# The last stores of a two-layer encoder trunk, issued by row halves from two engines

## What is computed

```python
def reference(x, p, ...):
    for i in range(DEPTH):                      # DEPTH = 2
        z = _rmsnorm(x, pre_norm_g[i]) @ w_in[i]
        ...                                     # both attentions, gated: oa, ob
        y = jnp.concatenate([oa * jax.nn.silu(ga), ob * jax.nn.silu(gb)], axis=-1) @ w_out[i]
        x = x + _rmsnorm(y, post_norm_g[i])
        gate = jax.nn.sigmoid(x @ w_ple_gate[i])
        e = (p[i] @ w_ple_proj[i]) * gate
        x = x + _rmsnorm(e, ple_norm_g[i])
    return x                                    # (1, 256, 1024) f32, 1 MB
```

## Time and profile before

| | before |
|---|---|
| median of 3 runs | 357.34 us (357.05 to 357.71) |
| the profiled execution | 356.97 us |
| its span, from first to last instruction | 355.2 us |
| around the span | 1.77 us |
| TensorE busy | 347.7 us, 98% of the span |
| granted TensorE clock, mean | 0.994 of full speed |
| DMA, mean over the span | 172 GB/s, 61.12 MB |
| of it written to memory | 1.05 MB |

### The profile page before, as it was taken

The page is one execution under the profiler, slowest core; times in us unless marked ns, Lnnn a source line. Parts: engine busy times, 40 slices in busy tenths (PEclk is TensorE's granted clock), DMA queues, the critical chain, the costliest instruction groups (busy, mean ns, idle before and its releaser), DMA issues.

```text
span 355.2 us, 5701 instructions
## 1 busy us (share of the span) xinstructions
PE 347.7 (98%) x1927; PEld 291.6 (82%) x1927; DVE 263.2 (74%) x562; ACT 228.9 (64%) x459; POOL 68.1 (19%) x121
## 2 busy tenths in 40 slices
PE   8999999999999999999999999999999999999992
PEld 7887888888888788888888888888888888888882
DVE  3886979988765776786697487998897458678543
ACT  4897566777578955555757564788666795465221
POOL 1076540142200000013106534014220000000000
PEclk9999999999999999999999999999999999999997
DMA  8996797662753364657575926546356346550011
GB/s 291 380 339 203 78 315 231 176 179 66 215 190 124 122 224 128 223 149 156 181 227 159 352 89 200 159 120 187 109 164 194 119 127 230 177 171 9 2 49 69
DMA packets 31820, 61.12 MB, mean 172 GB/s; under 512 B 2376, under 2 KB 4432, under 8 KB 31792
## 3 DMA queue, kind: packets, MB, share of 16 engines
q1 hardware_dynamic: 30656, 57.48, 49.9%
q0 software_dynamic: 1120, 3.28, 5.1%
q10 hardware_dynamic: 16, 0.00, 0.0%
HBM read 59.71 MB, written 1.05 MB: 171 GB/s over the span
## 4 chain that ended last, share of the span: by engine, by line
PE 96%; issue 2%; DVE 1%; ACT 0%; POOLq 0%; DVEq 0%; POOL 0%
PE proj L1256 25%; PE proj L1258 25%; PE proj L1257 25%; PE sc L1337 3%; PE tr L1407 2%; PE tr L1355 2%; PE pv L1424 2%; PE sc L1189 1%; PE proj L1173 1%; PE proj L1200 1%; PE pv L1429 1%; PE proj L1189 1%; PE pv L1189 1%; PE proj L1162 1%; PE sc L1207 1%
## 5 line engine op out<-in xcount | busy, mean ns | idle before, releaser
L1256 PE MATMUL proj<-w_hi,act_hi 128*128 128x512 f32 (+1 forms) x392 | 157.1, 401 | 0.0
L1258 PE MATMUL proj<-w_hi,act_lo 128*128 128x512 f32 (+1 forms) x392 | 152.2, 388 | 0.0
L1257 PE MATMUL proj<-w_lo,act_hi 128*128 128x512 f32 (+1 forms) x392 | 151.6, 387 | 0.0
L854 DVE TENSOR_TENSOR w_lo<-raw,w_hi 128x1024 fp32r<-128x1024 f32 (+1 forms) x102 | 121.2, 1209 | 14.3 <-ACT w_hi L612 13.7
L612 ACT ACTIVATE w_hi<-raw 128x1024 fp32r<-128x1024 f32 (+2 forms) x103 | 102.3, 1023 | 2.6 <-PE proj L1258 1.8
L1258 PEld LDWEIGHTS proj<-w_hi,act_lo 128*128 128x128 f32 x392 | 73.6, 188 | 15.5
L1256 PEld LDWEIGHTS proj<-w_hi,act_hi 128*128 128x128 f32 x392 | 73.7, 188 | 14.1 <-issue 0.7
L1257 PEld LDWEIGHTS proj<-w_lo,act_hi 128*128 128x128 f32 x392 | 73.9, 188 | 12.9
L552 POOL TENSOR_TENSOR rstd<-var,minus_half 128x1 f32<-128x1 f32 x12 | 7.6, 640 | 190.1 <-DVE var L842 161.4
L748 ACT ACTIVATE probs<-probs,neg_max 128x128 f32<-128x128 f32 (+1 forms) x64 | 28.2, 443 | 5.2 <-DVE neg_max L1005 5.2
L542 POOL TENSOR_TENSOR v_all<-work,rot_tab 128x128 f32<-128x128 f32 x16 | 10.6, 662 | 76.0 <-ACT work L612 75.8
(11 more groups left out here) (225 smaller groups left out, 455.6 us busy)
## 6 DMA issues: line engine op xcount, KB each, us to landing
raw<-in_w_in_dram SPq DMA_DIRECT2D x59, 512.0 KB, 4.3
raw<-in_w_out_dram SPq DMA_DIRECT2D x16, 512.0 KB, 3.4
raw<-in_w_ple_gate_dram SPq DMA_DIRECT2D x16, 512.0 KB, 3.7
raw<-in_w_in_dram SPq DMA_DIRECT2D x7, 324.0 KB, 5.5
raw<-in_w_ple_proj_dram SPq DMA_DIRECT2D x4, 512.0 KB, 3.9
resid<-in_x_dram SPq DMA_DIRECT2D x2, 512.0 KB, 6.6
probs<-in_w_in_dram SPq DMA_DIRECT2D x2, 512.0 KB, 9.3
g_ple<-in_ple_norm_g_dram POOLq DMA_DIRECT2D x2, 512.0 KB, 5.2
```

The costliest lines, as they stand in the source:

```text
L854: nc.vector.tensor_tensor(w_lo[:, g % SLOTS, 0:nk * cols], landing(g, nk * cols), w_hi[:, g % SLOTS, 0:nk * cols].bitcast(fp32), ALU.subtr ...
L1256: nc.tensor.matmul(ps, src_hi[:, b, k0 + k, :], hi, start=(first_u and k == 0), stop=False)
L1257: nc.tensor.matmul(ps, src_hi[:, b, k0 + k, :], lo, start=False, stop=False)
L1258: last = nc.tensor.matmul(ps, src_lo[:, b, k0 + k, :], hi, start=False, stop=last_k)
```

## The change

The two stores of row block 1 are cut in two by rows. The sync engine stores partitions 0 to 63 (rows 128 to 191) of each column half, and ScalarE stores partitions 64 to 127 (rows 192 to 255) from its own DMA queue, at the end of its list, each after a wait for the same count of `x2_done`. A new semaphore, `stored_low`, counts ScalarE's two stores, and the sync engine waits for it after `stored`. The stores of block 0 are as before.

```diff
-        eg_done, stored = sem("eg_done"), sem("stored")
+        eg_done, stored, stored_low = sem("eg_done"), sem("stored"), sem("stored_low")
@@ sync engine
             for i in range(2 * NB):
                 b, n = divmod(i, 2)
                 sp.wait_ge(x2_done, (DEPTH - 1) * 4 + i + 1)
-                sp.dma_start(out[0, b * P:(b + 1) * P, n * N:(n + 1) * N], resid[:, b, n * N:(n + 1) * N])\
+                rows = P if b == 0 else P // 2
+                sp.dma_start(out[0, b * P:b * P + rows, n * N:(n + 1) * N], resid[0:rows, b, n * N:(n + 1) * N])\
                     .then_inc(stored, 16)
             sp.wait_ge(stored, 16 * 2 * NB)
+            sp.wait_ge(stored_low, 16 * 2)
@@ ScalarE, in its list of steps
+                elif kind == "last":
+                    for n in range(2):
+                        act.wait_ge(x2_done, L * 4 + 3 + n)
+                        nc.scalar.dma_start(out[0, P + P // 2:2 * P, n * N:(n + 1) * N],
+                                            resid[P // 2:P, 1, n * N:(n + 1) * N]).then_inc(stored_low, 16)
```

## The result

| | before | after |
|---|---|---|
| median | 357.36 us (356.73 to 357.71, 6 runs) | 358.53 us (357.84 to 358.75, 6 runs) |
| ratio of the times | | 1.0031, 95% interval 1.0016 to 1.0046 |
| the profiled execution | 356.97 us | 357.84 us |
| its span | 355.2 us | 356.0 us |
| tail: end of VectorE's last update to end of span | 355.16 - 352.70 = 2.46 us | 356.00 - 352.65 = 3.35 us |

The changed kernel is slower by 0.3%, 0.6 to 1.6 us by the interval. The forecast was 357.36 us with a range up to 358.0, and "slower by over 0.2%" had a chance of 0.10.

The account below looks back on a forecast made before the run. TensorE holds 96% of the 355.2 us span; the change reaches only the 2.5 us tail of stores. Terms -0.02 + 0 + 0 + 0.02 + 0.02 + 0 = +0.02 us on 357.34 gave 357.36 us, range 356.95 to 358.0.

Parts of the forecast that it names:

- (4): Block 1's stores: four transfers have 64 small packets instead of 32; +0.02 us, bounds 0 and 0.04.
- (6): Final barrier: ScalarE's drain starts later but the wait for the sync engine covers it; 0, without cover 0.54 us.
- (5): Kernel end: the sync engine's additional wait; +0.02 us, bounds 0 and 0.05.
- (1): Sync engine's block 1 issues shrink from 128 rows to 64, so the first packet comes earlier; -0.02 us, bounds -0.04 and 0.
- (3): Block 1's store data: same bytes on the same full DMA engines, 0; a half alone at half rate costs 0.12 us more.
- half-rate rival: Block 1's half-row transfers run at half rate, one queue after the other; +1.37 us, 358.7 us, chance 0.08.
- (2): ScalarE issues the other halves of block 1, starting level with the sync engine; 0, at worst +0.24 us.
- late ScalarE: Rival: ScalarE's block 1 stores are late, the last half landing 0.24 to 0.36 us later; 357.6 to 357.7 us, chance 0.12.

Follow-up runs that it names:

- e2: Against the kernel before: block 1 stored as four transfers of 64 neighbouring rows, all from the sync engine; 358.76 us, ratio 1.0043, tail 3.98 us.
- e12: Against the kernel before: block 1 stored by the sync engine as 48, 80, 64 and 64 rows; one profiled execution, tail 3.58 us.
- e1: The changed kernel unaltered, run again and compared with the kernel before; 358.60 us, ratio 1.0034, tail 3.47 us.
- e5: Against the kernel before: block 1 stored as four transfers of 64 even or odd rows, all from the sync engine; 358.77 us, ratio 1.0032, tail 3.89 us.
- e8: The changed kernel with row halves swapped (sync engine partitions 64 to 127, ScalarE 0 to 63); 358.65 us, ratio 1.0040 to the kernel before, tail 3.47 us.
- e9: The changed kernel with even rows from the sync engine, odd rows from ScalarE; 357.72 us, ratio 1.0014 to the kernel before, tail 3.08 us.
- e10: The changed kernel with only ScalarE's half of block 1 stored, rows 128 to 191 left out; one profiled execution, data 1.40 us at 187 GB/s.
- e3: Against the kernel before: block 1's second column half, all 128 rows, stored by ScalarE, the first by the sync engine; 357.49 us, ratio 0.9999, tail 2.57 us.
- e4: Against the kernel before: both column halves of block 1, 128 rows each, stored by ScalarE; 357.63 us, ratio 1.0004, tail 2.59 us.
- e6: Against the kernel before: block 1 stored as four transfers of 128 rows by 256 columns, all from the sync engine; 358.13 us, ratio 1.0017, tail 3.05 us.
- e7: Against the kernel before: block 1 stored as four transfers of 128 rows by 256 columns, by sync engine and ScalarE; 357.74 us, ratio 1.0008, tail 2.76 us.

## Why the prediction was wrong

**What held.** The reading of the tail (2.5 us, all of it behind VectorE's last update), and parts (4) and (6): the data end 0.83 us before the end of the span before and 0.88 after. ScalarE's drain starts at 353.5 and is over long before the barrier. (5) can't be told apart. Two of the prediction's own signs of being wrong came: about 200 GB/s while one queue alone was moving, and queue 10's first packet 0.6 us behind queue 1's.

**Part (1) had the wrong sign.** The step from "128 rows are 332 ns, 256 rows are 367 ns" to "64 rows save 18 ns" took a straight line through two points and went on below them. An issue of 64 rows takes 548 ns (e2, e12). The first packet follows about 1.2 us after the issue's start in seven profiles (after, e1, e2, e5, e8, e9, e10) and 0.83 to 0.87 us with 128 rows (before, e3, e4, e6, e7). I had -0.02 us with bounds of -0.04 and 0; it was +0.36, and it alone takes half of the 0.71 us that I called invisible. The longer issue is 548 - 332 = 216 ns of it. The other 0.15 us lie behind the issue's end, where the first packet comes after 0.65 us with 64 rows and after 0.50 with 128 (before, e4); the prediction had no term for that.

**Part (3) and the half-rate rival were treated as an either-or.** I priced half rate at +1.37 us for all four transfers in turn, gave it 0.08, and let it go with the remark that two halves side by side fill each other's gaps. In the changed kernel they are not side by side at the start: queue 10 began only as queue 1's half ended, as the lines by queue show. My evidence for mixing was one stretch of the opening, in which one of the two transfers was 4 KB. So the first half went alone at 201 GB/s, and the last one, with nothing left beside it, ended alone at 215. In between the rate was mostly 380 to 420. The cost is +0.48 us of data, and e9, which has all of the change but the neighbours, has +0.03. I had only 0.12 for it, in part (3), as a bound. Why the halves in the middle escape I can only argue: by then both queues hold packets for different partitions, so the reads of one may run ahead under the other's. e2 (199 GB/s) and e10 (187), where no other queue is there, are slow from end to end, which fits.

**Part (2).** The late ScalarE was a wrong worry as put, since its 575 ns is no property of a queue long unused (e3, e4). It was late for another reason: its packets waited for the slow half of queue 1, and its last landing came after 2.9 us. Its second issue took 786 ns, but that is not seen to cost anything: in e9 it takes 799 and no gap follows.

**The sum.** +0.36 for the first packet (64 rows), +0.48 for the data (neighbours) and +0.05 behind them. That is 0.89 us of tail. The measured 1.17 us of the medians has an interval of 0.6 to 1.6 and doesn't contradict it.

**The chances.** Two costs, each under 0.71 us, add up to more than that. I weighed each rival alone against the threshold and gave no chance to a bit of two of them. The range's upper end of 358.0 came from one late store and should have added the half-rate stretches.

No run beat the kernel before. e3 and e4 tie with it: the issuing engine is free to choose, the cut isn't.

## What to carry to other kernels

A store at the end of a kernel is a lag, a stretch of data and a landing; if the data of one transfer already hide the issue of the next, a second issuer has nothing to save. Best don't cut it; if it must be cut, do it by columns and keep all 128 partitions, which cost 0.30 us with two issuers and 0.59 with one. A part of the partitions, if they are neighbours, draws about half the rate when no other queue runs beside it, and 64 rows were slower to issue than any other number tried. A price for a new shape of transfer doesn't come from a line through two other shapes; where no row has the shape, the bounds must reach to the slowest issue in the trace.

## What the runs showed of the hardware

- 64 rows of 2 KB: an issue of 0.52 to 0.61 us from either engine, neighbours or strided (0.57 to 0.80 from ScalarE with the sync engine issuing beside it), against 0.33 to 0.38 for 128 rows and 0.34 to 0.45 for 16, 32, 48, 80, 96 and 112.
- First packet after the issue's start: 1.2 us with 64 rows, 0.83 to 0.87 with 128.
- 64 neighbouring partitions alone: 187 to 205 GB/s, with the DMA engines counted as 0.81 to 0.96 busy; every second partition: 369 to 389. A high DMA share doesn't say that the rate is full.
- Two queues with a transfer of 2 KB rows each: the second starts when the first has moved nearly all its bytes (e9: 0.34 us later, without a gap). With 1 KB rows (e7) packets of both run side by side.
- An issue close behind another of the same engine takes 0.42 to 0.45 us instead of 0.33 to 0.34, which sets the pace of transfers of 128 KB.
